# Attention by pairs of heads with alternately issued products, and a shorter chain ahead of the experts' first gate product

## The reference

```python
def first_block(...):                        # DEPTH = 2 layers
    for l in range(DEPTH):
        q_a, k_a, v_a, u_b, cq_c, ckv_c, kpe_c, gate_logits = split(rms_norm(x, g_mix[l]) @ w_in[l])
        y_a = swa_attention(q_a, k_a, v_a, sinks[l], bias, mask)   # 8 heads of 64, window 128, T5 bias, sink
        y_b = conformer_conv(u_b, ...)                              # 31 taps, layer norm, swish
        y_c = mla_attention(cq_c, ckv_c, kpe_c, ...)                # 8 heads: 64 plain + 32 rotary features
        x = x + sum_n(sigmoid(gates_n) * (y_n @ w_branch[l, n])) @ w_out[l]
        x = x + square(relu(rms_norm(x, g_mlp[l]) @ w_up[l])) @ w_down[l]
    return rms_norm(x, g_final)

def second_block(x, c, ctx, ...):
    for i in range(DEPTH):
        # i = 0: retention and neighbourhood attention (8 heads of 64, window keys and context keys)
        # i = 1: pooling over positions, then four small products
        h = post_norm(h, m[2] * y, ...)
        h = post_norm(h, m[5] * hier_moe(modulate(h, ...)), ...)    # 32 experts, 2 of one group a token
    return h
```

## Time and profile before

| | |
|---|---|
| time of three runs, us | 2302.24, 2303.23, 2305.12 (median 2303.23) |
| the profiled execution, us | 2303.52 |
| its span, first to last instruction, us | 2301.7 |
| mean granted TensorE clock | 0.977 |
| PE busy | 2154.9 us, 94% |
| DVE busy | 983.0 us, 43% |
| ACT busy | 534.2 us, 23% |

### The profile page before, as it was taken

One profiled execution on the slowest core, in us unless ns is written; L12 is line 12 of the kernel. 1 busy time (PEld: TensorE's weight loads), 2 busy tenths in 40 slices (PEclk: granted clock), 3 DMA queues, 4 the chain that ended last, 5 costly groups with the idle time before them and its releaser, 6 DMA issues.

```text
span 2301.7 us, 30845 instructions
## 1 busy us (share of the span) xinstructions
PE 2154.9 (94%) x12800; PEld 1487.9 (65%) x12800; DVE 983.0 (43%) x2018; ACT 534.2 (23%) x976; POOL 3.1 (0%) x10
## 2 busy tenths in 40 slices
PE   7999899999999999999999799999987799999986
PEld 6876679998877779999986544443334544443332
DVE  7899536552168335556456521211112521221112
ACT  2112113331122114344234311111112211111111
POOL 0000000000000000000000000000000000000000
PEclk9999899999999999999998899999999899999999
DMA  6435364446433474443241699999999399999994
GB/s 263 155 138 220 146 255 184 182 183 256 165 128 147 173 289 161 183 163 109 95 164 48 265 417 425 427 425 429 426 426 426 138 419 426 428 425 429 425 425 206
DMA packets 50548, 621.05 MB, mean 270 GB/s; under 512 B 5616, under 2 KB 5616, under 8 KB 12560
## 3 DMA queue, kind: packets, MB, share of 16 engines
q1 hardware_dynamic: 49968, 615.79, 65.6%
q0 software_dynamic: 480, 3.87, 0.4%
HBM read 618.59 MB, written 1.05 MB: 269 GB/s over the span
## 4 chain that ended last, share of the span: by engine, by line
PE 67%; DMA 18%; DVE 12%; ACT 1%; issue 1%; DVEq 0%; SPq 0%; ACTq 0%
PE bank L615 19%; DMA ring<-in_experts 12%; PE bank L1251 10%; PE bank L1274 6%; DMA arena<-in_experts 6%; DVE wide L1888 3%; PE bank L818 3%; PE bank L819 3%; PE bank L820 3%; PE sums L820 3%; PE sums L819 3%; PE sums L818 3%; DVE arena L1915 3%; PE sums L615 2%; PE sums L1284 2%; PE bank L959 2%
## 5 line engine op out<-in xcount | busy, mean ns | idle before, releaser
L615 PE MATMUL bank<-h,ring 128*128 128x256 f32 x1568 | 348.4, 383 | 0.0
L615 PEld LDWEIGHTS bank<-h,ring 128*128 128x128 f32 x1568 | 298.2, 191 | 49.1 <-issue 7.3
L2130 DVE TENSOR_TENSOR ring_split<-ring,arena_split 128x2048 fp32r<-128x2048 f32 x64 | 144.2, 2289 | 151.1 <-ACT arena_split L1516 150.8
L2576 DVE TENSOR_TENSOR wide<-bank,wide 128x256 f32<-128x256 f32 x64 | 27.2, 425 | 398.7 <-ACT wide L1706 398.7
L2583 DVE SCALAR_TENSOR_TENSOR scratch_split<-bank,small,wide_split 128x512 fp32r<-128x512 f32 x64 | 48.0, 751 | 272.3 <-ACT wide_split L1714 272.3
L1516 ACT ACTIVATE arena_split<-ring 128x2048 fp32r<-128x2048 f32 x64 | 119.3, 1906 | 158.3 <-PE sums L820 144.0
L818 PE MATMUL bank<-h_split,arena_split 128*128 128x256 f32 x512 | 147.0, 287 | 6.7 <-DVE scratch_split L2153 6.7
L1251 PE MATMUL bank<-ring,h 128*64 128x512 f32 x640 | 143.6, 594 | 9.6 <-DMA ring<-in_experts 9.6
L819 PE MATMUL bank<-scratch_split,arena_split 128*128 128x256 f32 x512 | 146.1, 285 | 0.0
L820 PE MATMUL bank<-h_split,ring_split 128*128 128x256 f32 x512 | 146.0, 285 | 0.0
L818 PE MATMUL sums<-smax_split,arena_split 128*128 128x256 f32 x512 | 144.9, 283 | 0.0
(11 more groups left out here) (363 smaller groups left out, 3673.4 us busy)
## 6 DMA issues: line engine op xcount, KB each, us to landing
ring<-in_stream SPq DMA_DIRECT2D x99, 2048.0 KB, 7.8
ring<-in_experts SPq DMA_DIRECT2D x96, 2048.0 KB, 32.7
arena<-in_experts SPq DMA_DIRECT2D x72, 2048.0 KB, 31.2
arena<-in_experts SPq DMA_DIRECT2D x24, 1024.0 KB, 28.6
stat<-in_experts SPq DMA_DIRECT2D x24, 512.0 KB, 29.3
scratch<-in_experts SPq DMA_DIRECT2D x24, 512.0 KB, 31.0
arena<-in_stream SPq DMA_DIRECT2D x1, 2048.0 KB, 35.6
wide<-in_na_bias POOLq DMA_DIRECT2D x1, 1536.0 KB, 11.2
```

The costliest lines, as they stand in the source:

```text
L615: mm = pe.matmul(dst, a, b, start=(first and i == 0), stop=(i == len(terms) - 1))
L2130: dve.tensor_tensor(split["ring"][:, slot, 2048 * part:2048 * part + 2048], v, HI[("up", "down")[part]][:, j % 2, :].bitcast(F32), ALU.sub ...
```

## The change

1. The layers' attention runs over pairs of heads. `scores(l, pair)` opens two banks and issues the products of the even and the odd head alternately; both turns follow each other; `weigh(l, pair)` alternates between the heads too, and has two products a head, of 256 and 128 columns, in place of three of 128. ACT runs both exponentials of a pair ahead of its gates and turns. The turned probabilities have four buffers instead of two (two in `scratch`). The gate and modulation chunks stay with their units.
2. Neighbourhood attention: ACT keeps the first and second part of `nq` ahead of the copy of `rg`; PE's first eight units wait for the first part of `nq` alone; DVE adds the mask head by head inside the loop, and one of the two `ab_low` moves into it, behind unit 3.
3. Experts: the rank products take float32r operands (copies of the constants are made in `route`); slot numbers count from 1, so that ranks need no correction; two steps of the number of rounds go; `place` comes ahead of the register load; the first expert of each group of four waits for gathered tiles pair by pair; the banks of the first gathers are sorted.

```diff
-        member = smax[:, 0, 64:128].rearrange("p (t e) -> p t e", t=2)
+        member_r = split["smax"][:, 0, 64:128].rearrange("p (t e) -> p t e", t=2)
+        member = member_r.bitcast(F32)
+        counters = split["smax"][:, 0, 192:448]
...
+        def turned_at(u):
+            return smax[:, 4 + u % 2, :] if u % 4 < 2 else flat2(scratch[:, 2 * (u % 2):2 * (u % 2) + 2, :])
...
+                us = (2 * pair, 2 * pair + 1)
+                if pair == 0:
+                    S.wait(pe, "latent_keys", l)
+                    S.wait(pe, "latent_queries", l)
+                    S.wait(pe, "latent_rotated", l)
+                if pair == HEADS // 2:
+                    S.wait(pe, "window_queries", l, 1)
+                    S.wait(pe, "window_keys", l)
+                opened = [open_bank(pe, "s", l, u) for u in us]
+                terms = []
+                for u in us:
...
-                    if u == 0:
-                        S.wait(pe, "latent_keys", l)
-                        S.wait(pe, "latent_queries", l)
-                        S.wait(pe, "latent_rotated", l)
-                    pairs = [(A["qn"][a:a + HD, u // 2, :], A["kn"][a:a + HD, u // 2, :]),
-                             (A["qp"][b:b + 32, u // 4, :], A["kp"][b:b + 32, :])]
-                else:
-                    a = (u % 2) * HD
-                    if u == HEADS:
-                        S.wait(pe, "window_queries", l, 1)
-                        S.wait(pe, "window_keys", l)
-                    pairs = [(A["qa"][a:a + HD, (u - HEADS) // 2, :], A["ka"][a:a + HD, :])]
+                    if u < HEADS:
+                        terms.append([(A["qn"][a:a + HD, u // 2, :], A["kn"][a:a + HD, u // 2, :]),
+                                      (A["qp"][b:b + 32, u // 4, :], A["kp"][b:b + 32, :])])
+                    else:
+                        terms.append([(A["qa"][a:a + HD, (u - HEADS) // 2, :], A["ka"][a:a + HD, :])])
...
-                    mm = product(bank[:, c0:c1], [(q[:, t * P:(t + 1) * P], k[:, 0:nk]) for q, k in pairs])
-                filled(mm, "s", l, u)
+                    last = len(terms[0]) - 1
+                    for n in range(last + 1):
+                        for u, bank, pairs in zip(us, opened, terms):
+                            q, k = pairs[n]
+                            mm = pe.matmul(bank[:, c0:c1], q[:, t * P:(t + 1) * P], k[:, 0:nk], start=(n == 0), stop=(n == last))
+                            if t and n == last:
+                                filled(mm, "s", l, u)
...
-            state = {}
...
-            def weigh(l, u):
-                if u % 2 == 0:
-                    state["y"] = open_attended(l, u // 2)
-                S.wait(pe, "probs_turned", l, u)
-                bank, a = state["y"], (u % 2) * HD
-                v, c = (A["vc"], u * HD) if u < HEADS else (A["va"], a)
-                pT = smax[:, 4 + u % 2, :]
-                product(bank[a:a + HD, 0:P], [(v[:, 0, c:c + HD], pT[:, 0:P])])
-                mm = product(bank[a:a + HD, P:T], [(v[:, 0, c:c + HD], pT[:, P:T]), (v[:, 1, c:c + HD], pT[:, T:3 * P])])
-                if u % 2 == 1:
-                    filled(mm, "y", l, u // 2)
-                else:
-                    S.give(mm, "weighed", l, u)
+            def weigh(l, pair):
+                us = (2 * pair, 2 * pair + 1)
+                bank = open_attended(l, pair)
+                for u in us:
+                    S.wait(pe, "probs_turned", l, u)
+                for n in range(2):
+                    for u in us:
+                        a, pT = (u % 2) * HD, turned_at(u)
+                        v, c = (A["vc"], u * HD) if u < HEADS else (A["va"], a)
+                        if n == 0:
+                            pe.matmul(bank[a:a + HD, 0:T], v[:, 0, c:c + HD], pT[:, 0:T], start=True, stop=False, skip_group_check=True)
+                        else:
+                            mm = pe.matmul(bank[a:a + HD, P:T], v[:, 1, c:c + HD], pT[:, T:3 * P], start=False, stop=True,
+                                           skip_group_check=True)
+                            if u % 2:
+                                filled(mm, "y", l, pair)
+                            else:
+                                S.give(mm, "weighed", l, u)
...
-                for u in range(2 * HEADS + 3):
-                    if u < 2 * HEADS:
-                        scores(l, u)
-                    if u in GATE_UNITS:
-                        in_pair(l, GATE_UNITS[u])
-                    if u in MOD_UNITS[l]:
-                        mod_site(l, MOD_UNITS[l][u])
-                    if 2 <= u < 2 * HEADS + 2:
-                        turn(l, u - 2)
-                    if u >= 3:
-                        weigh(l, u - 3)
+                for pair in range(HEADS + 2):
+                    if pair < HEADS:
+                        scores(l, pair)
+                    for u in (2 * pair, 2 * pair + 1):
+                        if u in GATE_UNITS:
+                            in_pair(l, GATE_UNITS[u])
+                        if u in MOD_UNITS[l]:
+                            mod_site(l, MOD_UNITS[l][u])
+                    if 1 <= pair <= HEADS:
+                        turn(l, 2 * pair - 2)
+                        turn(l, 2 * pair - 1)
+                    if pair >= 2:
+                        weigh(l, pair - 2)
...
-                    pe.wait_ge(S.sem("projected"), S.value("projected", "nq", 1))
...
+                if u in (0, 8):
+                    pe.wait_ge(S.sem("projected"), S.value("projected", "nq", u // 8))
...
-                product(bank[:, 0:32], [(cst("before"), member[:, 0, :])])
-                product(bank[:, 32:64], [(ones, member[:, 0, :]), (cst("before"), member[:, 1, :])])
-                filled(product(bank[:, 64:96], [(ones, member[:, 0, :]), (ones, member[:, 1, :])]), "rank", i)
+                earlier, every = counters[:, 0:P], counters[:, P:2 * P]
+                product(bank[:, 0:32], [(earlier, member_r[:, 0, :])])
+                product(bank[:, 32:64], [(every, member_r[:, 0, :]), (earlier, member_r[:, 1, :])])
+                filled(product(bank[:, 64:96], [(every, member_r[:, 0, :]), (every, member_r[:, 1, :])]), "rank", i)
...
-                first_banks = [S.of("bank", "rows", i, t, half)[1] for half in range(2) for t in range(2)]
+                first_banks = [b for half in range(2) for b in sorted(S.of("bank", "rows", i, t, half)[1] for t in range(2))]
...
-                    if e == 0:
-                        raised("gather_kept", it, 4, 4)
...
+                            if e == 0 and k % 2 == 0:
+                                raised("gather_kept", it, k // 2 + 1, 4)
...
-                if u >= 2:
-                    S.wait(act, *weighed(l, u - 2))
-                ins = act.activation(smax[:, 4 + u % 2, 0:n], bank[:, 0:n], ACT.Copy)
+                back = 2 if l == "na" else 4
+                if u >= back:
+                    S.wait(act, *weighed(l, u - back))
+                at = smax[:, 4 + u % 2, :] if l == "na" else turned_at(u)
+                ins = act.activation(at[:, 0:n], bank[:, 0:n], ACT.Copy)
...
-                for u in range(2 * HEADS + 3):
-                    if u < 2 * HEADS:
-                        softmax_exps(l, u)
-                    if u in GATE_UNITS:
-                        tanh_gates(l, GATE_UNITS[u])
-                    if 2 <= u < 2 * HEADS + 2:
-                        turned(l, u - 2, 3 * P)
-                    if u >= 4 and u % 2 == 0:
-                        attended(l, (u - 4) // 2)
+                for pair in range(HEADS + 2):
+                    if pair < HEADS:
+                        softmax_exps(l, 2 * pair)
+                        softmax_exps(l, 2 * pair + 1)
+                    for u in (2 * pair, 2 * pair + 1):
+                        if u in GATE_UNITS:
+                            tanh_gates(l, GATE_UNITS[u])
+                    if 1 <= pair <= HEADS:
+                        turned(l, 2 * pair - 2, 3 * P)
+                        turned(l, 2 * pair - 1, 3 * P)
+                    if pair >= 2:
+                        attended(l, pair - 2)
...
+            keep("nq")
...
-            keep("nq")
...
-            ab_low(C_ABOUT, 1, 1)
+            def mask_bias(hd):
+                v = W2["nbias"][:, hd, :].rearrange("p (e c) -> p e c", c=GRID)
+                link(dve.tensor_tensor(v, v, cst("na_mask").unsqueeze(1).to_broadcast([P, 6, GRID]), ALU.add))
...
-            nb = W2["nbias"].rearrange("p h (e c) -> p (h e) c", c=GRID)
-            m = cst("na_mask").unsqueeze(1).to_broadcast([P, 48, GRID])
-            link(dve.tensor_tensor(nb, nb, m, ALU.add))
+            mask_bias(0)
...
+                if u % 2 == 0 and u < 14:
+                    mask_bias(u // 2 + 1)
+                if u == 3:
+                    ab_low(C_ABOUT, 1, 1)
...
+                dve.tensor_copy(counters[:, 0:P], cst("before"))
```

(26 more changed lines are left out.)

4 lines of the change are left out of this document (1 added, 3 removed).

## The result

The changed kernel takes 2276.5 us (median of 4, 2273.4 to 2276.8), the kernel before 2302.7 beside it: ratio 0.9881, 95% interval 0.9869 to 0.9893, which is 27.4 us less (the two medians are 26.2 apart). The forecast was 2281.5 (2271 to 2291). The profiled execution is the fastest of the four, 2273.4 (span 2271.6); about 3 of the 30.1 us between the two spans are its own.

What follows compares the result with a forecast made beforehand. DVE bounds layer 0's attention, PE layer 1's until about 731 us, and DMA the experts from 1497 us. 2303.5 + 0.7 (layer 0) - 12.9 (layer 1) - 4.6 (neighbourhood) - 5.2 (first gates) = 2281.5 us, range 2271 to 2291.

Steps and rivals of the forecast that it cites:

- Layer 0, +0.7: Attention of layer 0: DVE hides PE's saving, its period stays; weighing two pairs at the tail adds 0.7 us.
- PE's saving in layer 1, 17.8: Layer 1's attention: alternated products fully overlap (lower bound), and fewer changes of form at 0.19 us each; PE saves 17.8 us.
- New waits, +9.5: Layer 1's attention: PE waits 2.6, 4.1 and 2.8 us before pairs 4, 5 and 6, 9.5 us together.
- old ones, -4.9: Layer 1's attention: PE's old waits near 731 and 760 us, 4.9 us in the walk, go.
- The clock in layer 1, "I take no difference": Layer 1's attention: the granted clock fell twice in the old order; the forecast took no difference from it.
- R1: Layer 1's attention: waits and the clock take back half, so it gives -6 us; total 2288 us, chance 0.25.
- R2: Product pairs of attention: alternating is no overlap, each pays 0.19 us, layer 1 gives about +4; about 2298 us, chance 0.08.
- R3: Both attention layers: pairs starve DVE, 3 us a boundary; layer 0 loses 21, layer 1 gains nothing; 2315 us, chance 0.05.
- R4: More than forecast: no fall of the clock in layer 1, none at the neighbourhood heads; 2270 us, chance 0.12.
- Neighbourhood heads, -4.6: Neighbourhood stage: earlier first turn, fuller DVE loop and less time at the lower clock sum to -4.6 us, bounds -1 and -8.
- "-2.2" for the first turn: Neighbourhood stage: PE's output product sets the first turn, which comes at 1210.0 instead of 1212.25 us.
- Ahead of the first gates, -5.2: Both expert stages: shorter way to the first gate product, -2.3 and -2.9 us, together -5.2, bounds -3 and -7.

Runs made afterwards that it cites:

- Experiment 5: Changed kernel with ACT's order within a pair as exponential of the even head, its tanh, exponential of the odd head, tanh: 2279.0 us, 0.9890 to the kernel before.
- experiment 6: Changed kernel with layer 1's conv taps dealt out as 18, 12, 18, 12, 12, then 6 a head: 2267.5 us, 0.9841 to the kernel before.
- experiments 7 and 8: Changed kernel with a latent pair's score products sorted by height, 2275.4 us; changed kernel with weighing in three products of 128 columns a head, 2277.3 us.
- experiment 4: Changed kernel with the even head's score and weighing products all issued before the odd head's: 2293.8 us, 0.9948 to the kernel before.
- experiments 9 and 10: Changed kernel with layer 1's taps dealt out anew and latent score products sorted by height, 2266.5 us; the same with the neighbourhood edits undone, 2268.5 us.

## Why the prediction was right or wrong

**Sign and range** were right: 27.4 us less where 21.7 were forecast, counted from the median. The size came in part by luck: layer 1 gave more than its term and the neighbourhood part less (alone 20.5 against 12.2, and 1.6 against 4.6), and the two errors partly cancel. The terms, by the two profiled executions and by the parts alone:

- *Layer 0, +0.7:* nothing against it, but too small to tell. Layer 1's first scores start at 639.94 against 639.98; in all thirteen traces they start between 639.65 and 645.61. DVE's period held, as the forecast said it must.
- *PE's saving in layer 1, 17.8:* right. 4 x 2.06 + 4 x 0.85 + 8 x 0.80 = 18.0. PE's time in the stage without its waits, and with time at half rate counted half, went from 118.5 to 100.6 us, 17.9 less. The lower bound for the alternated products (full overlap) was the true value, and so was the price of a change of form. The Trainium skill (TensorEngine Tiling (Array Packing), "Key Properties") says that switching the tiling mode drains the engine and that tiles work independently; the trace agrees with both: 0.195 us a change, and two heads in the time of one.
- *New waits, +9.5, old ones, -4.9:* right in place, 8.1 and 4.1 measured, so +4.0 instead of +4.6. What the waits come from was not right. The forecast named ACT's order, the tanh behind both exponentials. Experiment 5 took that away and the time stayed; experiment 6 moved DVE's taps and 6.8 us of waits went. DVE's taps stood in the same chain, and a walk through the program order gave the right microseconds under the wrong name. The forecast set against it that "DVE has 20 us of slack" over the first 91 us; in the kernel before that slack lay in gaps of 1.7 to 3.4 us ahead of latent heads, and from 706.15 to 739.5, over the last latent head and the first window heads, DVE had no gap above 0.5 us.
- *The clock in layer 1, "I take no difference":* this is the mis-sized term. The kernel before has two falls of 6.8 us there, the changed one, the one with the pairs alone and experiment 5 a single one of 3.4, experiments 7 and 8 two of 3.4, and those with the taps moved none. At half rate and not in a wait, PE spent 11.4 us in the kernel before and 3.4 in the changed one; half of that is what it cost, 5.7 and 1.7 us, so the clock gave 4.0. The forecast put it at nothing, and with the saving and the waits it makes up the 17.9 measured (17.9 - 4.0 + 4.0). Rival R1 (more half rate after the new waits, 0.25) went the other way: of waits of 2.5, 4.1 and 1.4 us, only the second was followed by a fall. The case that the Trainium skill describes (TensorE: Matmul & The Clock Gate, "HAM oscillation — how this bites in real kernels") has waits of about 3 to 5 us between bursts of matmuls, and each of them brings the half rate back. Of the waits of layer 1 in the kernels by pairs, the two of 4.1 us did so (the changed kernel and the pairs alone), and none of 1.2 to 1.5 us did. Of eight waits of 2.5 to 3.0 us, five were followed by a fall (experiments 5, 7 and 8) and three were not (the changed kernel, the pairs alone, and experiment 4, whose wait of 3.0 us is the longest of the eight).
- *R2 (alternating is no overlap)* is out by the rows of the changed kernel, a latent pair in 2.10 us where experiment 4 has 4.16, and *R3 (the pairs starve DVE)* by the unchanged period of layer 0. R4 asked for no fall in layer 1 and none at the neighbourhood heads; neither was quite so.
- *Neighbourhood heads, -4.6:* too large; 1.6 (-0.7 to 3.7) alone, and 1.8 us between experiments 9 and 10 (0.9839 against 0.9847), whose intervals overlap. Of its terms, "4 us earlier" for the first scores came with this part alone; in the changed kernel it was 2.7. "-2.2" for the first turn failed. In the changed kernel it was 1.1: the output product started 7.3 us behind the projections, where the forecast's 1203.9 means 5.9. In the other kernels with the edits the half rate fell on that product, which sets the turn. That "of the 13.7 us at the lower clock (cost about 6.9) I let half go" came true in the changed kernel and with the part alone, but the time at half rate is between 3.4 and 13.7 us with the edits and between 6.8 and 13.7 without.
- *Ahead of the first gates, -5.2:* 2.0 + 3.8 = 5.8 in the trace and 7.1 (4.4 to 10.1) alone. Rank to `place` gave 1.8 and 2.4 (forecast 1.35 and 2.0).

What stays open: some 4 us of the profiled difference lie behind the first gate of the first stage (1.5 in the pooling, 2.3 in the last expert stage and the tail, where the kernel before has falls of the clock that the changed one lacks). The profiled execution is 3.2 us faster than its kernel's median, so some 3 of them may be its own, and no experiment touched them.

## What to carry to other kernels

When a change makes the bounding engine faster, ask by stretches, not over the stage, whether the next engine has slack; a filler loop that was harmless (12 taps a head) is then on the path, and dealing it out to where its engine idles can be worth a third as much as the change itself (9 of 27 us). In this kernel two heads on two halves of the rows or columns overlapped in either order of issue where the height stayed the same, and only alternated where it changed; so alternate where the height changes, and don't count on it for more elsewhere. A walk through the program order finds the size and place of a wait, but to name its cause, remove the candidate.

## What was unexpected of the hardware

- Window heads issued one after the other overlapped as fully as alternated ones (0.86 us a pair both ways), latent ones not at all (4.16 against 2.10).
- The clock fell without an idle engine: in experiment 4 it fell at 645.7, 686.6 and 703.7, where PE had not been idle for more than 0.7 us. Each fall began 2.6 to 3.5 us after the start of a latent pair's scores, issued head by head on half of the rows or fewer; the scores at 664.14 brought none. The kernel before has such scores in pieces of 2.1 us, and no fall there in layer 1. The rows of the first fall:

```profile
642.69 5.22 PE L736 MATMUL bank<-arena 64*128 64x128 f32 x16 [0.69 <-ACT arena L1397]
...
645.70:652.50 6.80, 6.80 (x15) 4.61 (x16) 6.66 (x23) 1.06 (x5) 0.00 (x0) 0.50 0.43 181
```

- In the changed kernel's layer 1, waits of 2.5 and 1.4 us brought no fall and one of 4.1 us a fall of 3.4 us, while in the kernel before waits of 1.3 and 2.0 us came with falls of 6.8 us each.
